# Split float32 products: one 512-column matmul for both halves of the activations

## The chip, the cores and the metric

One core of one Trainium2 chip runs the whole program. The metric is device time in microseconds, the median of several executions; lower is better.

## The reference

Two models in a row on 256 tokens of width 1024, in float32. The first block is a mixer (convolution branch, SSM branch, gates) followed by a mixture of 64 experts; the second is two layers, each with three mixing branches, an output projection and a feed-forward net with a squared ReLU. The places that matter here:

```python
# first block, end of the mixer
y_cv = u @ w_cv_out
y_ssm = y.reshape(bsz, seq, D_INNER) @ w_ssm_out
return (g_cv * y_cv + g_ssm * y_ssm) @ w_mix_out
# second block, each of two layers
x = x + merged @ w_out[l]
h2 = rms_norm(x, norm2_g[l])
x = x + jnp.square(jax.nn.relu(h2 @ w_ff1[l])) @ w_ff2[l]
```

## The kernel before

Activations are kept transposed: 128 channels on the partitions, T = 256 tokens along the free dimension; a tile is 128x256. A weight matrix is the stationary operand in blocks of 128x128. Most products are plain float32 (`group`, L176). The products named above are *split products*: a float32 weight tile is split into a high half `wh` (rounded to the one-pass type fp32r by an ACT copy) and a low half `wl` (the rest, by a DVE subtraction), the activations likewise into `xh` and `xl`, and wh*xh + wl*xh + wh*xl is summed in one PSUM bank.

**A split product** has 8 k-tiles (16 in the SSM projection) of three matmuls of 256 columns: L483 to L485 in the mixer's tail (`mixer_pe`, `halved_product`), L1724 to L1726 in the layers (`layer_pe`, `halved_product`). It fills half a bank, `k.pb[b][:, 0:T]`:

```python
e.matmul(k.pb[b][:, 0:T], wh[:, kt, c0:c0 + 128], xh, start=(first and kt == 0), stop=False)
e.matmul(k.pb[b][:, 0:T], wl[:, kt, c0:c0 + 128], xh, start=False, stop=False)
ins = e.matmul(k.pb[b][:, 0:T], wh[:, kt, c0:c0 + 128], xl, start=False, stop=(last and kt == 7))
```

**Groups and queues.** Each engine's instruction list is written out by hand and runs in order; semaphores tie the engines. In a layer the split weights come in 18 groups j of 2 MB: j = 0 and 1 the output projection, 2 to 9 `w_ff1`, 10 to 17 `w_ff2`; a group of weights serves four products. Two buffers `parts` hold the split weights. SP loads group j + 2 into the raw buffer once `ff_low` of group j is done. At the start of turn j, ACT issues `ff_high(j + 1)` (two copies of 128x2048, L1798), which waits until the products of group j - 1 are done, and DVE issues `ff_low(j + 1)` (two subtractions of 128x2048, L1805). Then both work on the four products of group j, and PE starts group j + 1 when its `ff_low` is done.

**Emptying a bank in ff1** (j = 2 to 9): ACT writes relu (L2009), DVE first makes the low half of the product before (`hid_low`, L2296) and then squares relu (L2327), ACT makes the high half (`hid_high`, L2011):

```python
o.done(e.activation(v.relu[:, m % 2, :], k.pb[k.bank["ff", 72 * l + 8 + m]][:, 0:T], ACT.Relu), k.s("relu"))
e.wait_ge(*k.at("hid_sq", 32 * l + m + 1))
o.done(e.activation(v.high[m], v.hsq[:, m % 2, :], ACT.Copy), k.s("hid_high"))
```

In the output projection and in `w_ff2` DVE adds the bank to `k.h` (L2319, L2333), ACT squares the result for the next norm (L194) and PE sums the squares (L201). PE takes banks from a ring of seven; a bank is used again when the operation that emptied it has signalled.

**The mixer's tail** has the same scheme: 8 groups, 24 products (2, 2, 2, 2 of 16 k-tiles, then 4, 4, 4, 4 of 8), `tail_high` (L644) and `tail_low` (L653) for the weights. Products 0 to 7 are multiplied by a gate when emptied (L825), 8 to 15 multiplied by a gate and added (L827, L828) and split (`yc_high` L613, `yc_low` L812); products 16 to 23 take the result as their input and go into `k.h` (L832). Just ahead of products 0 to 3 DVE finishes `uc_low` (L808), the input of products 8 to 15.

Of the kernel before, what the change touches and what calls it, by code (L numbers as in the profile page):

```python
# [215 lines left out]


# [75 lines left out]
class Mix:  # L293


    def __init__(self, k):
# [45 lines left out]
def mixer_pe(k, e, emptied):  # L342
# [133 lines left out]
    def halved_product(n, w, c0, x, kt, late):  # L476

        b = ring.take(("tail", n))
        (wl, wh), (xl, xh) = w, x
        for j in range(kt):  # L480
            if late:
                e.wait_ge(*k.at(late, 8 * j // kt + 1))
            e.matmul(k.pb[b][:, 0:T], wh[:, j, c0:c0 + 128], xh[:, j, :], start=(j == 0), stop=False)  # L483
            e.matmul(k.pb[b][:, 0:T], wl[:, j, c0:c0 + 128], xh[:, j, :], start=False, stop=False)  # L484
            ins = e.matmul(k.pb[b][:, 0:T], wh[:, j, c0:c0 + 128], xl[:, j, :], start=False, stop=(j == kt - 1))  # L485
        ins.then_inc(k.s("mm_tail"), 1)
        return b
# [168 lines left out]
def mixer_ve(k, e, o):  # L656
# [158 lines left out]
    for j in range(8):  # L815
# [4 lines left out]
        for n in range(TAIL_GROUPS[j - 1] if j else 0, TAIL_GROUPS[j]):  # L820
            acc = k.pb[k.bank["tail", n]][:, 0:T]
            e.wait_ge(*k.at("mm_tail", n + 1))
            m = n % 8
            if n < 8:
                o.done(e.tensor_tensor(m_.yc[:, m, :], acc, g[:, 8 + m, :], ALU.mult), k.s("tail"))  # L825
            elif n < 16:
                t = o.done(e.tensor_tensor(m_.tmp[:, m % 2, :], acc, g[:, m, :], ALU.mult), k.s("tail"))  # L827
                o.done(o.after(t).tensor_tensor(m_.yc[:, m, :], m_.yc[:, m, :], m_.tmp[:, m % 2, :], ALU.add), k.s("yc"))  # L828
                if m:
                    yc_low(m - 1)  # L830
            else:
                o.done(e.scalar_tensor_tensor(k.h[:, m, :], acc, k.mod[:, 16 + m:17 + m], k.h[:, m, :], ALU.mult, ALU.add), k.s("tail"))  # L832
# [510 lines left out]
class Layer:  # L1343


    def __init__(self, k, l):
# [41 lines left out]
        self.relu, self.hsq = k.tiles(80, 2), k.tiles(82, 2)  # L1388
# [93 lines left out]
def layer_pe(k, e, l, emptied_by):  # L1482
# [233 lines left out]
    def halved_product(b, j, i, x, first, last, late=None, late_from=0):  # L1716
# [767 lines left out]
```

## Time and profile before

| | us |
|---|---|
| median of 3 runs | 2615.01 (2614.14 to 2616.16) |
| the profiled execution | 2613.7 |
| its span, first to last instruction | 2611.9 |
| PE busy | 2179.4 (83%) |
| DVE busy | 1026.4 (39%) |
| ACT busy | 679.0 (26%) |
| mean granted TensorE clock | 0.908 |

The profiled execution's time is 1.8 us more than its span. A clock of 1.0 is 2.4 GHz, 0.5 is 1.2 GHz. PE is the matrix engine and PEld its weight loads, DVE the vector engine, ACT the scalar engine. An engine's busy time counts overlapping matmuls once. The split products run from 390 to 490 us (mixer's tail), 1825 to 2048 (layer 0) and 2385 to 2606 (layer 1); between lie the experts, whose weights stream from memory, and the plain float32 parts.

### The profile page before, as it was taken

How to read it: one execution, taken by the hardware profiler on the slowest of the kernel's cores; microseconds unless marked ns; L12 is line 12 of the kernel's file. 1: busy time of each engine (PE TensorE's matmuls, PEld its weight loads, DVE VectorE, ACT ScalarE, POOL GpSimd, SP SyncE). 2: the span in 40 equal slices, each digit the busy share in tenths (PEclk: the TensorE clock that was granted, in tenths of full speed). 3: DMA queues.
4: the chain of work that ended last, by engine and by line, in shares of the span. 5: the costliest groups of instructions: out<-in, count | busy, mean ns of one | idle time of the engine just before them, and what ended most of it. 6: DMA issues, size and time to landing. Idle time of an engine off the chain costs nothing.

```text
span 2611.9 us, 31851 instructions
## 1 busy us (share of the span) xinstructions
PE 2179.4 (83%) x13027; PEld 1589.9 (61%) x13027; DVE 1026.4 (39%) x2106; ACT 679.0 (26%) x1048; POOL 27.3 (1%) x47
## 2 busy tenths in 40 slices
PE   7999999867667666777666588989899988899999
PEld 4886679833223333333333265778899855688999
DVE  1577865510010000101000246763664267653653
ACT  2125665300000000000000123641453125522542
POOL 0000000000000000000000010000000200000000
PEclk8999999887887888788888799999999989899999
DMA  8443544499999999999999613233355322143452
GB/s 323 150 143 133 196 155 162 198 396 421 422 389 421 421 421 421 421 421 421 421 420 422 255 48 122 99 111 129 133 190 189 114 83 104 65 160 131 158 177 101
DMA packets 174501, 631.45 MB, mean 242 GB/s; under 512 B 10816, under 2 KB 28768, under 8 KB 125200
## 3 DMA queue, kind: packets, MB, share of 16 engines
q1 hardware_dynamic: 173008, 628.07, 61.1%
q8 instruction: 106, 1.74, 0.3%
q0 software_dynamic: 1344, 1.28, 0.3%
q14 instruction: 43, 0.35, 0.0%
HBM read 628.28 MB, written 1.05 MB: 241 GB/s over the span
## 4 chain that ended last, share of the span: by engine, by line
PE 55%; DMA 27%; DVE 10%; ACT 4%; SPq 2%; issue 2%; DVEq 0%; ACTq 0%
DMA ring<-in_w 26%; PE pb L176 23%; PE pb L1724 5%; PE pb L1725 5%; PE pb L1726 5%; PE pb L1022 4%; PE pb L1048 3%; SPq L935 2%; DVE ar L2231 1%; PE pb L485 1%; PE pb L484 1%; PE pb L483 1%; PE pb L1681 1%; DMA ring<-in_w_ada 1%; PE pb L201 1%
## 5 line engine op out<-in xcount | busy, mean ns | idle before, releaser
L176 PE MATMUL pb<-ar,ring 128*128 128x256 f32 (+1 forms) x2960 | 673.5, 387 | 32.1 <-DVE ar L2033 18.0
L176 PEld LDWEIGHTS pb<-ar,ring 128*128 128x128 f32 (+1 forms) x2960 | 561.4, 192 | 138.6 <-issue 43.6
L1022 PE MATMUL pb<-ring,ar 128*32 128x512 f32 x2048 | 283.7, 710 | 125.0 <-DMA ring<-in_w 124.4
L1724 PE MATMUL pb<-act,parts 128*128 128x256 f32 x1152 | 331.2, 287 | 13.3 <-DVE act L2309 13.3
L1725 PE MATMUL pb<-act,parts 128*128 128x256 f32 x1152 | 327.7, 284 | 0.0
L1726 PE MATMUL pb<-act,parts 128*128 128x256 f32 x1152 | 327.6, 284 | 0.0
L1048 PE MATMUL pb<-ring,ar 128*32 128x512 f32 x1024 | 174.2, 842 | 114.2 <-DMA ring<-in_w 114.2
L1022 PEld LDWEIGHTS pb<-ring,ar 128*32 128x32 f32 x2048 | 77.6, 127 | 309.7 <-issue 309.0
L1724 PEld LDWEIGHTS pb<-act,parts 128*128 128x128 f32 x1152 | 221.7, 192 | 14.5 <-issue 14.1
L1725 PEld LDWEIGHTS pb<-act,parts 128*128 128x128 f32 x1152 | 221.6, 192 | 0.4
L1726 PEld LDWEIGHTS pb<-act,parts 128*128 128x128 f32 x1152 | 221.6, 192 | 0.0
L1805 DVE TENSOR_TENSOR parts<-ring,parts 128x2048 fp32r<-128x2048 f32 x72 | 161.7, 2288 | 107.0 <-ACT parts L1798 107.0
L1048 PEld LDWEIGHTS pb<-ring,ar 128*32 128x32 f32 x1024 | 46.3, 147 | 230.1 <-issue 226.4
L1245 DVE TENSOR_TENSOR ar<-ar,pb 128x512 f32<-128x512 f32 x16 | 11.0, 687 | 432.4 <-PE pb L1022 432.4
L1099 ACT ACTIVATE ar<-pb 128x512 f32<-128x512 f32 x16 | 9.6, 597 | 598.8 <-PE pb L1048 598.8
L176 PE MATMUL pb<-ar 128*128 128x128 f32 x512 | 126.5, 423 | 44.7 <-DVE ar L1222 42.5
L176 PEld LDWEIGHTS pb<-ar 128*128 128x128 f32 x512 | 123.4, 335 | 59.0 <-DVE ar L1222 56.7
L1798 ACT ACTIVATE parts<-ring 128x2048 fp32r<-128x2048 f32 x72 | 133.5, 1901 | 79.4 <-PE pb L1726 76.6
L1253 DVE COPY ar<-pb 128x512 f32<-128x512 f32 x16 | 11.1, 692 | 277.8 <-PE pb L1048 277.8
L693 DVE SCALAR_TENSOR_TENSOR ar<-ar,par 128x256 f32<-128x256 f32 x240 | 104.5, 476 | 0.0
L1093 ACT ACTIVATE ar<-pb 128x512 f32<-128x512 f32 x16 | 9.6, 597 | 319.8 <-PE pb L1022 319.8
L176 PE MATMUL pb<-ring,ar 128*128 128x512 f32 (+3 forms) x304 | 75.3, 427 | 14.4 <-DVE ring L2148 14.4
(355 smaller groups left out, 2393.4 us busy)
## 6 DMA issues: line engine op xcount, KB each, us to landing
ring<-in_w SPq DMA_DIRECT2D x384, 1024.0 KB, 18.7
ring<-in_w_in SPq DMA_DIRECT2D x36, 2048.0 KB, 7.7
ring<-in_w_ff SPq DMA_DIRECT2D x32, 2048.0 KB, 8.7
ring<-in_w_ada SPq DMA_DIRECT2D x12, 2048.0 KB, 12.1
ring<-in_w_ssm_out SPq DMA_DIRECT2D x4, 2048.0 KB, 8.2
ring<-in_w_out SPq DMA_DIRECT2D x4, 2048.0 KB, 7.7
ring<-in_w_cv_out SPq DMA_DIRECT2D x2, 2048.0 KB, 8.2
ring<-in_w_mix_out SPq DMA_DIRECT2D x2, 2048.0 KB, 7.6
```

What stands on the lines that cost most here:

```text
L176: ins = e.matmul(out, l, r, start=(i == 0), stop=(i == len(pairs) - 1))
L201: e.matmul(k.pb[SUMS][:, 0:T], k.con("ones"), k.tiles(85 + g % 2, 1)[:, 0, :], start=first, stop=last).then_inc(k.s("squared_sum"), 1)
L483: e.matmul(k.pb[b][:, 0:T], wh[:, j, c0:c0 + 128], xh[:, j, :], start=(j == 0), stop=False)
L693: made[m] = o.done(e.scalar_tensor_tensor(uc[:, m, :], ut[:, m, j:j + T], cw[:, m, j:j + 1], uc[:, m, :], ALU.mult, ALU.add), k.s("taps") ...
L935: e.dma_start(half_slot(k, n, [128, kt, 2048 // kt]), src).then_inc(k.s(f"expert{n % HALVES}"), 16)
L1022: ins = e.matmul(k.pb[b][32 * j:32 * j + 32, :], v.xg[i][:, kt, 32 * j:32 * j + 32], w[j][:, m, :], start=(kt == 0), stop=(kt == 7))
L1048: ins = e.matmul(k.pb[yb[c]][32 * j:32 * j + 32, :], v.ht[i][:, kt, 32 * j:32 * j + 32], w[j][:, m, 512 * c:512 * c + 512], start=(kt == 0 ...
L1724: e.matmul(k.pb[b][:, 0:T], wh[:, kt, c0:c0 + 128], xh, start=(first and kt == 0), stop=False)
L1725: e.matmul(k.pb[b][:, 0:T], wl[:, kt, c0:c0 + 128], xh, start=False, stop=False)
L1726: ins = e.matmul(k.pb[b][:, 0:T], wh[:, kt, c0:c0 + 128], xl, start=False, stop=(last and kt == 7))
L1798: o.done(o.e.activation(high[:, 4 * i:4 * i + 4, :], raw[:, 4 * i:4 * i + 4, :], ACT.Copy), k.s("ff_high"))
L1805: o.done(o.e.tensor_tensor(low[:, 4 * i:4 * i + 4, :], raw[:, 4 * i:4 * i + 4, :], high[:, 4 * i:4 * i + 4, :].bitcast(F32), ALU.subtract) ...
```

## The change

The high and low halves of a tile of activations become one moving operand of 512 columns (`pair`, two tiles at a distance). `wh` multiplies both at once into a full bank of 512 columns, and `wl` multiplies the high half into the columns where wh*xh stands. The bank then holds two partial sums, which are added when it is emptied.

```diff
--- before.py
+++ after.py
@@ -214,6 +214,27 @@
     return k.tiles(88, 1)[:, 0, :]
+class Both:
+    def __init__(self, k, high, low):
+        a, b = min(high, low), max(high, low)
+        self.pair, self.high, self.at = k.act[:, a:b + 1:b - a, :], k.act[:, high, :], T * (high > low)
+def halved_products(e, acc, wh, wl, x, first, last):
+    both = acc[:, :].rearrange("p (t n) -> p t n", t=2)
+    if last:
+        e.matmul(acc[:, x.at:x.at + T], wl, x.high, start=False, stop=False)
+        return e.matmul(both, wh, x.pair, start=first, stop=True)
+    e.matmul(both, wh, x.pair, start=first, stop=False)
+    return e.matmul(acc[:, x.at:x.at + T], wl, x.high, start=False, stop=False)
 FIRST_FILLS = 2
@@ -310,7 +331,11 @@
         self.xdt = [k.scratch(9 + 4 * i, 1024).rearrange("p (t h c) -> p t h c", t=2, h=8) for i in range(2)]
         self.ucl, self.uch, self.zl, self.zh = k.act[:, 8:16, :], k.act[:, 72:80, :], k.act[:, 40:56, :], k.act[:, 24:40, :]
         self.yc, self.tmp = k.tiles(16, 8), k.tiles(82, 2)
+        self.tmp2 = k.tiles(80, 2)
         self.ycl, self.ych = k.act[:, 16:24, :], k.act[:, 0:8, :]
+        self.zb = [Both(k, 24 + m, 40 + m) for m in range(16)]
+        self.ucb = [Both(k, 72 + m, 8 + m) for m in range(8)]
+        self.ycb = [Both(k, m, 16 + m) for m in range(8)]
 def halves(k, j, shape):
@@ -476,24 +501,22 @@
     def halved_product(n, w, c0, x, kt, late):
         b = ring.take(("tail", n))
-        (wl, wh), (xl, xh) = w, x
+        wl, wh = w
         for j in range(kt):
             if late:
                 e.wait_ge(*k.at(late, 8 * j // kt + 1))
-            e.matmul(k.pb[b][:, 0:T], wh[:, j, c0:c0 + 128], xh[:, j, :], start=(j == 0), stop=False)
-            e.matmul(k.pb[b][:, 0:T], wl[:, j, c0:c0 + 128], xh[:, j, :], start=False, stop=False)
-            ins = e.matmul(k.pb[b][:, 0:T], wh[:, j, c0:c0 + 128], xl[:, j, :], start=False, stop=(j == kt - 1))
+            ins = halved_products(e, k.pb[b], wh[:, j, c0:c0 + 128], wl[:, j, c0:c0 + 128], x[j], j == 0, j == kt - 1)
         ins.then_inc(k.s("mm_tail"), 1)
         return b
     for j in range(8):
         e.wait_ge(*k.at("low", 2 * j + 2))
         if j < 4:
-            w, x, cols, kt, late = halves(k, j, [16, 256]), (m_.zl, m_.zh), 2, 16, "z_low"
+            w, x, cols, kt, late = halves(k, j, [16, 256]), m_.zb, 2, 16, "z_low"
         elif j < 6:
-            w, x, cols, kt, late = halves(k, j, [8, 512]), (m_.ucl, m_.uch), 4, 8, "uc_low"
+            w, x, cols, kt, late = halves(k, j, [8, 512]), m_.ucb, 4, 8, "uc_low"
         else:
-            w, x, cols, kt, late = halves(k, j, [8, 512]), (m_.ycl, m_.ych), 4, 8, "yc_low"
+            w, x, cols, kt, late = halves(k, j, [8, 512]), m_.ycb, 4, 8, "yc_low"
         for i in range(cols):
             n = (TAIL_GROUPS[j - 1] if j else 0) + i
             b = halved_product(n, w, 128 * i, x, kt, late)
@@ -818,18 +841,25 @@
         if 2 <= j < 7:
             tail_low(k, o, j + 1)
         for n in range(TAIL_GROUPS[j - 1] if j else 0, TAIL_GROUPS[j]):
-            acc = k.pb[k.bank["tail", n]][:, 0:T]
+            acc = [k.pb[k.bank["tail", n]][:, T * i:T * i + T] for i in range(2)]
             e.wait_ge(*k.at("mm_tail", n + 1))
             m = n % 8
+            tmp = m_.tmp[:, m % 2, :]
             if n < 8:
-                o.done(e.tensor_tensor(m_.yc[:, m, :], acc, g[:, 8 + m, :], ALU.mult), k.s("tail"))
+                o.done(e.tensor_tensor(m_.yc[:, m, :], acc[0], g[:, 8 + m, :], ALU.mult))
+                t = o.done(e.tensor_tensor(tmp, acc[1], g[:, 8 + m, :], ALU.mult), k.s("tail"))
+                o.done(o.after(t).tensor_tensor(m_.yc[:, m, :], m_.yc[:, m, :], tmp, ALU.add))
             elif n < 16:
-                t = o.done(e.tensor_tensor(m_.tmp[:, m % 2, :], acc, g[:, m, :], ALU.mult), k.s("tail"))
-                o.done(o.after(t).tensor_tensor(m_.yc[:, m, :], m_.yc[:, m, :], m_.tmp[:, m % 2, :], ALU.add), k.s("yc"))
+                t1 = o.done(e.tensor_tensor(tmp, acc[0], g[:, m, :], ALU.mult))
+                t2 = o.done(e.tensor_tensor(m_.tmp2[:, m % 2, :], acc[1], g[:, m, :], ALU.mult), k.s("tail"))
+                t1 = o.done(o.after(t1).tensor_tensor(tmp, tmp, m_.yc[:, m, :], ALU.add))
                 if m:
                     yc_low(m - 1)
+                o.done(o.after(t1, t2).tensor_tensor(m_.yc[:, m, :], tmp, m_.tmp2[:, m % 2, :], ALU.add), k.s("yc"))
             else:
-                o.done(e.scalar_tensor_tensor(k.h[:, m, :], acc, k.mod[:, 16 + m:17 + m], k.h[:, m, :], ALU.mult, ALU.add), k.s("tail"))
+                h, gain = k.h[:, m, :], k.mod[:, 16 + m:17 + m]
+                t = o.done(e.scalar_tensor_tensor(h, acc[0], gain, h, ALU.mult, ALU.add))
+                o.done(o.after(t).scalar_tensor_tensor(h, acc[1], gain, h, ALU.mult, ALU.add), k.s("tail"))
 def mixer_po(k, e):
@@ -1385,7 +1415,10 @@
         self.nh, self.nl = k.act[:, 8:16, :], k.act[:, 16:24, :]
         self.high = [k.act[:, 24 + m, :] for m in range(32)]
         self.low = [k.act[:, (56 + m if m < 24 else m - 24), :] for m in range(32)]
-        self.relu, self.hsq = k.tiles(80, 2), k.tiles(82, 2)
+        self.hid, self.hsq, self.part = k.tiles(80, 2), k.tiles(82, 2), k.tiles(91, 2)
+        self.mgb = [Both(k, 68 + m, 60 + m) for m in range(8)]
+        self.nb = [Both(k, 8 + m, 16 + m) for m in range(8)]
+        self.hidb = [Both(k, 24 + m, 56 + m if m < 24 else m - 24) for m in range(32)]
 def unit_place(v, name):
@@ -1718,12 +1751,9 @@
         wl, wh = halves(k, j, [8, 512])
         c0 = 128 * i
         for kt in range(8):
-            xl, xh = x(kt)
             if late:
                 e.wait_ge(*k.at(late, late_from + kt + 1))
-            e.matmul(k.pb[b][:, 0:T], wh[:, kt, c0:c0 + 128], xh, start=(first and kt == 0), stop=False)
-            e.matmul(k.pb[b][:, 0:T], wl[:, kt, c0:c0 + 128], xh, start=False, stop=False)
-            ins = e.matmul(k.pb[b][:, 0:T], wh[:, kt, c0:c0 + 128], xl, start=False, stop=(last and kt == 7))
+            ins = halved_products(e, k.pb[b], wh[:, kt, c0:c0 + 128], wl[:, kt, c0:c0 + 128], x[kt], first and kt == 0, last and kt == 7)
         ins.then_inc(k.s("mm_ff"), 1)
     mid = SQ[f"mid{l}"]
@@ -1733,7 +1763,7 @@
             m = 4 * j + i
             b = wide.take(("ff", 72 * l + m))
             if j < 2:
-                halved_product(b, j, i, lambda kt: (v.mgl[:, kt, :], v.mgh[:, kt, :]), True, True, "mg_low", 8 * l)
+                halved_product(b, j, i, v.mgb, True, True, "mg_low", 8 * l)
                 wide.until(b, *k.at("h_mid", 8 * l + m + 1))
                 if m >= 2:
                     square_sum(k, e, mid + m - 2, ROOT[f"mid{l}"], m == 2, False)
@@ -1741,8 +1771,8 @@
                     square_sum(k, e, mid + 6, ROOT[f"mid{l}"], False, False)
                     square_sum(k, e, mid + 7, ROOT[f"mid{l}"], False, True)
             else:
-                halved_product(b, j, i, lambda kt: (v.nl[:, kt, :], v.nh[:, kt, :]), True, True, "n_low", 8 * l)
-                wide.until(b, *k.at("relu", 32 * l + m - 7))
+                halved_product(b, j, i, v.nb, True, True, "n_low", 8 * l)
+                wide.until(b, *k.at("hid", 32 * l + m - 7))
     for half in range(2):
         bs = [wide.take(("ff2", 8 * l + 4 * half + i)) for i in range(4)]
         for kb in range(4):
@@ -1750,7 +1780,7 @@
             e.wait_ge(*k.at("ff_low", 2 * (NSPLIT * l + j + 1)))
             e.wait_ge(*k.at("hid_low", 32 * l + 8 * kb + 8))
             for i in range(4):
-                halved_product(bs[i], j, i, lambda kt: (v.low[8 * kb + kt], v.high[8 * kb + kt]), kb == 0, kb == 3)
+                halved_product(bs[i], j, i, v.hidb[8 * kb:8 * kb + 8], kb == 0, kb == 3)
                 if kb == 3:
                     m = 4 * half + i
                     wide.until(bs[i], *k.at("h_out", 8 * l + m + 1))
@@ -2005,8 +2035,8 @@
                 m -= 8
                 e.wait_ge(*k.at("mm_ff", 72 * l + 8 + m + 1))
                 if m >= 2:
-                    e.wait_ge(*k.at("hid_sq", 32 * l + m - 1))
-                o.done(e.activation(v.relu[:, m % 2, :], k.pb[k.bank["ff", 72 * l + 8 + m]][:, 0:T], ACT.Relu), k.s("relu"))
+                    e.wait_ge(*k.at("hid", 32 * l + m - 1))
+                o.done(e.activation(v.part[:, m % 2, :], k.pb[k.bank["ff", 72 * l + 8 + m]][:, T:2 * T], ACT.Copy), k.s("part"))
                 e.wait_ge(*k.at("hid_sq", 32 * l + m + 1))
                 o.done(e.activation(v.high[m], v.hsq[:, m % 2, :], ACT.Copy), k.s("hid_high"))
             elif l == 0 and j in (13, 17):
@@ -2295,6 +2325,11 @@
         e.wait_ge(*k.at("hid_high", 32 * l + m + 1))
         return o.done(e.tensor_tensor(v.low[m], v.hsq[:, m % 2, :], v.high[m].bitcast(F32), ALU.subtract), k.s("hid_low"))
+    def add_halves(m, b, told):
+        h = k.h[:, m, :]
+        t = o.done(e.tensor_tensor(h, k.pb[b][:, 0:T], h, ALU.add))
+        o.done(o.after(t).tensor_tensor(h, k.pb[b][:, T:2 * T], h, ALU.add), k.s(told))
     low_done = [None, None]
     for j in range(NSPLIT):
         if j == 0:
@@ -2316,21 +2351,23 @@
             m = 4 * j + i
             if j < 2:
                 e.wait_ge(*k.at("mm_ff", 72 * l + m + 1))
-                o.done(e.tensor_tensor(k.h[:, m, :], k.pb[k.bank["ff", 72 * l + m]][:, 0:T], k.h[:, m, :], ALU.add), k.s("h_mid"))
+                add_halves(m, k.bank["ff", 72 * l + m], "h_mid")
             elif j < 10:
                 m -= 8
+                acc, hid = k.pb[k.bank["ff", 72 * l + 8 + m]], v.hid[:, m % 2, :]
+                e.wait_ge(*k.at("part", 32 * l + m + 1))
+                t = o.done(e.tensor_tensor(hid, acc[:, 0:T], v.part[:, m % 2, :], ALU.add), k.s("hid"))
                 if m:
                     low_done[(m - 1) % 2] = hid_low(m - 1)
-                e.wait_ge(*k.at("relu", 32 * l + m + 1))
                 if m >= 2:
                     o.after(low_done[m % 2])
-                o.done(e.tensor_tensor(v.hsq[:, m % 2, :], v.relu[:, m % 2, :], v.relu[:, m % 2, :], ALU.mult), k.s("hid_sq"))
+                o.done(o.after(t).scalar_tensor_tensor(v.hsq[:, m % 2, :], hid, 0.0, hid, ALU.max, ALU.mult), k.s("hid_sq"))
                 if m == 31:
                     hid_low(31)
             elif j in (13, 17):
                 m = 4 * (j // 17) + i
                 e.wait_ge(*k.at("mm_ff", 72 * l + (56 if j == 13 else 72) - 3 + i))
-                o.done(e.tensor_tensor(k.h[:, m, :], k.pb[k.bank["ff2", 8 * l + m]][:, 0:T], k.h[:, m, :], ALU.add), k.s("h_out"))
+                add_halves(m, k.bank["ff2", 8 * l + m], "h_out")
     if l:
         for n in range(4):
             if n % 2:
```

## Rows read from the trace of the kernel before

**Rows 1.** The page, busy time and share of the span: PE.
```profile
PE 2179.4 (83%) x13027; PEld 1589.9 (61%) x13027; DVE 1026.4 (39%) x2106; ACT 679.0 (26%) x1048; POOL 27.3 (1%) x47
```

**Rows 2.** The page, chain that ended last, by line: shares of the span.
```profile
DMA ring<-in_w 26%; PE pb L176 23%; PE pb L1724 5%; PE pb L1725 5%; PE pb L1726 5%; PE pb L1022 4%; PE pb L1048 3%; SPq L935 2%; DVE ar L2231 1%; PE pb L485 1%; PE pb L484 1%; PE pb L483 1%; PE pb L1681 1%; DMA ring<-in_w_ada 1%; PE pb L201 1%
```

**Rows 3.** Busy time by stage: layer 0, groups 2 to 9, and four microseconds of it.
```profile
core 0: us, PE busy (x) PEld busy (x) DVE busy (x) ACT busy (x) POOL busy (x), PEclk, DMA share, GB/s
1858.60:1953.30 94.70, 94.54 (x771) 94.57 (x772) 61.81 (x86) 51.57 (x80) 0.00 (x0) 0.97 0.46 166
1859.00:1863.00 4.00, 4.00 (x20) 4.00 (x21) 4.00 (x7) 3.33 (x2) 0.00 (x0) 0.50 0.01 2
```

**Rows 4.** Timeline of ACT, one group of ff1: start, length, instruction [idle before].
```profile
1931.39 3.71 ACT L1798 ACTIVATE parts<-ring 128x2048 fp32r<-128x2048 f32 x2
...
1938.59 0.42 ACT L2011 ACTIVATE act<-ar 128x256 fp32r<-128x256 f32 x1 [3.23 <-DVE ar L2327]
1938.91 0.37 ACT L2009 ACTIVATE ar<-pb 128x256 f32<-128x256 f32 x1
...
1942.58 0.42 ACT L2011 ACTIVATE act<-ar 128x256 fp32r<-128x256 f32 x1 [0.49 <-DVE ar L2327]
1942.90 1.90 ACT L1798 ACTIVATE parts<-ring 128x2048 fp32r<-128x2048 f32 x1
```

**Rows 5.** Timeline of DVE, the same group.
```profile
1937.80 0.42 DVE L2296 TENSOR_TENSOR act<-ar,act 128x256 fp32r<-128x256 f32 x1
1938.14 0.42 DVE L2327 TENSOR_TENSOR ar<-ar 128x256 f32<-128x256 f32 x1
...
1939.38 0.42 DVE L2327 TENSOR_TENSOR ar<-ar 128x256 f32<-128x256 f32 x1
```

**Rows 6.** Groups of instructions, shapes apart: count, busy us, mean ns, idle before.
```profile
L1724 PE MATMUL pb<-act,parts 128*128 128x256 f32 x1152 | 331.2, 287 | 13.3 <-DVE act L2309 13.3
...
L483 PE MATMUL pb<-act,parts 128*128 128x256 f32 x256 | 73.7, 288 | 0.0
...
L1724 PEld LDWEIGHTS pb<-act,parts 128*128 128x128 f32 x1152 | 221.7, 192 | 14.5 <-issue 14.1
...
L2264 DVE TENSOR_TENSOR ar<-ar 128x512 f32<-128x512 f32 x2 | 1.4, 684 | 0.0
...
L2267 DVE SCALAR_TENSOR_TENSOR ar<-ar 128x512 f32<-128x512 f32 x2 | 1.4, 682 | 0.0
```

**Rows 7.** The chain of work in order of time: start, length of the piece, what.
```profile
1740.43 1.72 PE pb L1660 x4
1742.15 82.88 PE pb L176 x384
...
1860.59 0.21 PE pb L1725
```

**Rows 8.** Timeline of PE: matmuls of one column, and the last transposes.
```profile
204.04 0.95 PE L337 MATMUL pb<-const,ring 128*128 128x1 f32 x8
...
2606.11 1.94 PE L171 MATMUL pb<-const,h 128*128 128x128 f32 x16 [0.61 <-DVE h L2333]
```

**Rows 9.** Timeline of DVE, mixer's tail: products 0 to 3, 5, 12, 15.
```profile
420.31 1.41 DVE L825 TENSOR_TENSOR ar<-pb,ar 128x256 f32<-128x256 f32 x4
...
430.24 0.42 DVE L825 TENSOR_TENSOR ar<-pb,ar 128x256 f32<-128x256 f32 x1 [3.64 <-PE pb L485]
...
460.86 0.42 DVE L827 TENSOR_TENSOR ar<-pb,ar 128x256 f32<-128x256 f32 x1
461.31 0.42 DVE L828 TENSOR_TENSOR ar<-ar 128x256 f32<-128x256 f32 x1
...
466.17 0.43 DVE L812 TENSOR_TENSOR act<-ar,act 128x256 fp32r<-128x256 f32 x1 [0.15 <-ACT act L613]
```

**Rows 10.** Timeline of PE in layer 1: the first matmul after an idle stretch.
```profile
2214.00 0.48 PE L176 MATMUL pb<-ar,ring 128*128 128x256 f32 x1 [2.79 <-ACT ar L1880]
```

**Rows 11.** Busy time and granted clock around that stretch, columns as in rows 3.
```profile
2210.00:2220.00 10.00, 7.21 (x33) 5.47 (x31) 8.10 (x19) 8.58 (x13) 0.00 (x0) 0.83 0.00 0
```

## The prediction

> **What bounds the kernel now.** I read the page's busy line first: PE is busy 83% of the span [rows 1]. The chain that ended last says which busy time counts [rows 2]: most is the load of MoE weights and full float32 products (L176), which the change does not touch; the reader should see that the three split products L1724 to L1726 hold 15% and L483 to L485 3%. The windows come next: in the stage of split products PE was busy 94.5 of 94.7 us at clock 0.97, DVE 61.8 and ACT 51.6 [rows 3]. So PE sets this stage, and a cheaper product seems to go straight to the time. But busy shares hide handshakes, so the timelines of ACT and DVE over one group of four products were read last [rows 4, 5]. The two `ff_high` of one group start at 1931.39, those of the next at 1942.90: 11.51 us for 96 matmuls, 0.120 each.
>
> **The matmuls.** There are 1152 + 256 = 1408 k-tiles of three [rows 6]: 0.360 us each. The change makes two matmuls of the three: 512 columns with `wh`, 256 with `wl`. Neither a 512-column nor any other size of this one-pass type is in the trace, so the pair is bounded. Float32 matmuls are recorded as two passes and take two array cycles a column: 82.88 us / 384 = 0.216 for 256 columns, 1.72 / 4 = 0.430 for 512 [rows 7]. So columns cost in proportion, and one pass of 512 one-cycle columns takes about 0.216, of 256 about 0.109 (as the 128-column two-cycle row: 1.94 us for 16, 0.109 apart after the first) [rows 8]. The measured 0.120 is more than 0.109. At the low clock of 0.5 [rows 3] the interval is 0.21 [rows 7], which is 256/1.2 with nothing added, so a fixed extra per matmul is unlikely. Loading 128 weight columns has a floor: matmuls of one column are (0.95-0.25-0.03)/6 = 0.112 apart [rows 8]. I take the 0.120 as a weight load running beside a matmul. Behind a 512-column matmul the next load is hidden, behind a 256-column one it is not: 0.216 + 0.120 = **0.336** a k-tile. Bounds: 0.325 if a load behind the short one costs only 0.109; 0.360 if 0.120 is a price per column (0.240 + 0.120), when nothing is gained. I take the middle because the floor of 0.112 lies near 0.120. A product of 8 k-tiles goes from 2.88 to 2.69 us (-0.19), a group of four from 11.52 to 10.75. All 1408 on the path would give 1408 x 0.024 = 33.8 us. They are not all on it.
>
> A load takes 0.192 us by its record, yet load and matmul repeat every 0.120 [rows 4, 6], so they run beside each other. The Trainium skill ("TensorE: Matmul & The Clock Gate", part 3, "What overlaps and what doesn't") says that a load overlaps a running matmul only when its row group differs. The trace disagrees, since all of these use all 128 rows; by the rule a dropped load would be worth its whole time, which is a rival below.
>
> **The added work in ff1** (groups j = 2 to 9, both layers). Before, for each product: ACT relu, DVE square, ACT `high`, and DVE `hid_low` of the product before. ACT and DVE wait for each other. After: ACT copies the second half (`part`), DVE adds the first (`hid`), then `hid_low`, then the square, then ACT `high`, and only then can ACT, in order, copy the next `part`. Steps, from rows: square to `high` 1938.59-1938.14 = 0.45; `high` to the next PSUM read 0.32 [rows 4, 5]; that read 0.37 and 0.03 until DVE starts = 0.40, no longer hidden behind `high`'s end; `hid` 0.335; `hid_low` to square 0.34 (1938.14-1937.80). Sum **1.85** a product against 1.24 before (1939.38-1938.14) [rows 5]. The square is now a scalar_tensor_tensor with a constant: that form takes 682 ns at 512 elements where tensor_tensor takes 684 [rows 6], so it costs nothing more.
> One turn of the loop, from one `ff_high` to the next: 6.41 until the split of the next weights lets DVE go on (1937.80-1931.39) + 0.335 + 0.34 + 3 x 1.85 + 0.45 + 0.32 = **13.4 us** [rows 4, 5]. Before, the same sum is 6.41 + 0.34 + 3 x 1.24 + 0.45 + 0.32 = 11.2, just under PE's 11.52, which is why no wait shows. After, 13.4 is over PE's 10.75: PE waits for the weights' low half, queued on DVE behind the `hid` work, and that is late next.
> How much arrives: the split has slack at first. From the last product of group 2 (E2), 1.9 to the first turn (0.04 + 0.37 + 0.03 + 0.335 + 0.34 + 0.45 + 0.32), then 7 turns of 13.4, then 6.5 to the low half of group 11, then its 10.75 and 0.2 of pipeline: E2 + 113.2. Before: 9 x 11.52 = 103.7. So **+9.5** a layer.
>
> **The rest of a layer.** Groups 0 to 2: 12 products x 0.192 = -2.3; the second DVE add at the end of the output projection is exposed, 0.42 + 0.04 = +0.46. Groups 12 to 17: 24 x 0.192 = -4.6, DVE and ACT only split weights there and the split keeps its slack. The last add: +0.46. Layer: 9.5 - 2.3 + 0.5 - 4.6 + 0.5 = +3.6, two layers **+7.2**. The wait for `part` is also queued in front of `hid_low` on DVE, but its `high` is done by then: nothing. The banks come free later, at `hid` in place of relu; a product waits for a bank used seven products earlier, so more than a group of slack covers it. DMAs are issued after `ff_low` as before, two groups ahead; the next turns are longer, so they are covered. ACT's instruction count does not change.
>
> **The mixer's tail** (256 k-tiles, products of 16 k-tiles 5.76 to 5.38). Products 0 to 3 are emptied in one go before the split for group 3: four at 0.33 become four chains mult, mult, add of 0.33 + 0.46 + 0.34 = 1.13. With products 0 to 2 done earlier this chain starts 0.8 earlier, at 419.5, the split then runs 424.1 to 428.5; PE wants it at 430.0 - 6 x 0.384 = 427.7 [rows 9]: stall 0.8. After eight products: -3.1 + 0.8 = -2.3. Products 8 to 15: a dependent pair 0.45 apart before (461.31-460.86); after, five DVE operations of 0.336 = 1.68 each. From the end of product 7: split done +6.45, four at 1.68 (+0.15 for the first), `high` 0.4, split of group 6 done at 19.7, four more, then the last `yc_low` at 27.4; product 16 needs it for its last k-tile and ends at 27.8. Before, it ended at 25.9 (9 x 2.88), the last `yc_low` starting at 466.17, half a microsecond early [rows 9]. +1.9. The other seven products -1.3, the second add at the end +0.5. Sum **-1.2**.
>
> **Sum:** 7.2 - 1.2 = +6.0 on the profiled execution's 2613.7 us (span 2611.9 and 1.8 around it). The median 2615.0 lies 1.3 above that execution: **2621.0**.
>
> **Rivals.** Faster and slower mean by over 0.2%, 5.2 us, about what a measurement of this kernel can tell.
> (a) 0.120 is per column. Then products gain nothing: a layer 10.3 + 0.5 + 0.5 = +11.3, the mixer's tail +1.9 + 0.5 = +2.4: +25, 2640. The same comes if the operand of two separate tiles is fetched more slowly or goes out as two instructions. For it: 0.120 is above the load's floor. Against: that floor is near. 20%.
> (b) 0.325 a k-tile: layer +9.2 - 3.4 + 0.5 - 6.7 + 0.5 = about 0, mixer -2: 2613, no change. 10%.
> (c) Faster: ACT and DVE are limited by work and not by the handshake. DVE's own work in a group is 4.4 + 4 x 1.01 = 8.5 us, ACT's 3.6 + 4 x 0.7 = 6.4, both under 10.75. Then PE sets ff1 too: a layer 72 x -0.192 + 0.9 = -12.9, the mixer -5.6: -31, 2584. It decides if the round is below (10.75 - 6.41 - 0.675 - 0.77)/3 = 0.96 us. Against it: even today's round is 1.24, and DVE waits for ACT and ACT for DVE in each. 5%.
> (d) A dropped load is worth its whole 0.112: 0.248 a k-tile, product 1.98. The loop of 13.4 still caps ff1: layer 6.7 - 10.3 - 21.0 = -24.6, mixer about -8: 2558. 1%. The overlap rule of the Trainium skill's page named above would bring this.
> (e) The clock: PE now idles 13.4 - 10.75 = 2.7 us in each turn. After an idle of 2.79 us at 2211 the ten microseconds around it had a mean clock of 0.83, so 3.4 us at the low level [rows 10, 11], 1.7 us lost, less than the 2.7 it idles. Twice as long costs 3.4, 0.7 more than the idle, in some 12 turns: +9, 2630. 6%.
>
> **How the numbers follow.** The forecast of 2621 has 58%. Its own error, 0.05 us in each step of the loop, is +-3 us, so some 18% of it lies under 2620.2 and is "same". With (b): same 0.28. Faster is (c), (d) and a little of (b): 0.08. Slower: 0.64. The range takes in (b) and (a): 2612 to 2640; (c) and (d) and tails are left out.
>
> **What the profile will show.** 1408 matmuls of 512 columns 0.216 apart from the next, 1408 of 256 at 0.120; `ff_high` pairs 13.4 us apart in groups 4 to 9, `part` starting 0.32 after `high`; PE waiting 2 to 3 us per group for L1805's line, none in groups 12 to 17; one PE wait of 3 to 4 us for the last `yc_low` in the mixer's tail. Wrong would be: 0.240 between long matmuls (a), turns of about 11 us (c), or a clock under 0.9 in ff1 (e).

## The result, and the profile after

| | before | after |
|---|---|---|
| median, us | 2615.59 (4 runs) | 2635.44 (4 runs, 2633.33 to 2637.39) |
| ratio to before | 1 | 1.0076, 95% interval 1.0064 to 1.0088 |
| profiled execution | 2613.7 | 2633.3 |
| its span | 2611.9 | 2631.5 |

The changed kernel is slower by 20 us, 0.76%. The page after, busy time and the chain by line:

```profile
PE 2167.4 (82%) x11619; PEld 1513.3 (58%) x11619; DVE 1073.5 (41%) x2242; ACT 677.0 (26%) x1048; POOL 27.3 (1%) x47
...
DMA ring<-in_w 26%; PE pb L176 22%; PE pb L232 7%; PE pb L1078 3%; PE pb L1052 3%; PE pb L233 3%; DVE parts L1835 3%; SPq L965 2%; ACT parts L1828 1%; DVE ar L2261 1%; PE pb L1714 1%; DVE ar L2364 1%; DVE ar L2359 1%; DMA ring<-in_w_ada 1%; PE pb L201 1%
```

There are 1408 fewer matmuls than in [rows 1], yet PE's busy time fell by 12 us only, and the chain has new members that [rows 2] has not: the weight split L1835 (`ff_low`, L1805 before), its ACT part L1828, the square L2364 and the new add L2359. The shapes, as in [rows 6]:

```profile
L232 PE MATMUL pb<-act,parts 128*128 128x512 f32 x1288 | 474.4, 408 | 30.2 <-DVE parts L1835 13.6 <-DVE act L2344 13.3 <-DVE act L2326 2.0
L233 PE MATMUL pb<-act,parts 128*128 128x256 f32 x1288 | 365.6, 284 | 0.0
...
L231 PE MATMUL pb<-act,parts 128*128 128x512 f32 x120 | 47.6, 397 | 0.0
L230 PE MATMUL pb<-act,parts 128*128 128x256 f32 x120 | 34.0, 283 | 0.6 <-DVE act L835 0.6
```

1288 + 120 = 1408 pairs, in one instruction each, as the change says. A long matmul, however, is not followed by the next at 0.216 us. The timeline of PE in ff1 of layer 0 (start, length, instruction, idle before):

```profile
1938.89 0.40 PE L232 MATMUL pb<-act,parts 128*128 128x512 f32 x1
1939.12 0.28 PE L233 MATMUL pb<-act,parts 128*128 128x256 f32 x1
1939.24 0.39 PE L232 MATMUL pb<-act,parts 128*128 128x512 f32 x1
...
1951.83 0.50 PE L232 MATMUL pb<-act,parts 128*128 128x512 f32 x1 [1.93 <-DVE parts L1835]
```

The starts are 0.235 and 0.117 apart (medians over all of them), 0.352 a k-tile: 0.008 less than the 0.360 of the three, not 0.024. The last row is PE's new wait at the start of a group, for the low half of its weights.

Where the 20 us are, by stage. Layers 0 and 1 of the changed kernel, from the end of group 0 to the ends of groups 2, 11 and 17 (busy time of PE, PEld, DVE, ACT, POOL, then the clock):

```profile
1841.20:1876.40 35.20, 27.97 (x144) 23.68 (x143) 23.59 (x39) 16.54 (x25) 0.00 (x0) 0.90 0.41 142
1876.40:1990.20 113.80, 105.89 (x578) 90.73 (x577) 75.60 (x127) 55.97 (x82) 0.00 (x0) 0.97 0.48 166
1990.20:2060.10 69.90, 69.90 (x395) 60.70 (x395) 29.91 (x34) 21.42 (x17) 0.00 (x0) 1.00 0.43 150
2408.00:2443.10 35.10, 27.87 (x143) 23.60 (x142) 23.59 (x39) 16.54 (x26) 0.00 (x0) 0.90 0.40 142
2443.10:2556.80 113.70, 106.03 (x577) 90.67 (x576) 71.88 (x106) 52.65 (x76) 0.00 (x0) 0.97 0.47 165
2556.80:2624.60 67.80, 67.80 (x385) 58.56 (x383) 28.22 (x24) 18.60 (x10) 0.00 (x0) 1.00 0.28 99
```

and the same stretches of layer 0 before:

```profile
1837.20:1872.50 35.30, 28.51 (x208) 27.48 (x207) 20.98 (x32) 16.65 (x25) 0.00 (x0) 0.90 0.40 145
1872.50:1976.20 103.70, 103.70 (x867) 103.70 (x866) 65.04 (x90) 56.80 (x82) 0.00 (x0) 1.00 0.49 176
1976.20:2047.40 71.20, 71.20 (x588) 70.94 (x587) 28.13 (x34) 21.41 (x17) 0.00 (x0) 1.00 0.43 154
```

The middle stretch carries it: 103.7 with PE busy all of it before, 113.8 with PE idle for 7.9 after. The stretch behind it is 1.3 shorter, the one ahead the same. From the end of group 0 to the end of group 17, layer 0 took 8.7 us more and layer 1 8.8. The mixer's tail, from the end of its first product to the end of its last, took 95.4 against 93.4, +2.0. The rest of the span adds up to +0.1: +0.2 ahead of the tail, +1.8 from the tail to layer 0 (mostly the stretch of experts, where the DMA engines are busy 0.99 of the time in both kernels, 948.5 us against 947.0), -2.4 between the layers (no run explains this one), +0.5 at the end, where the second add is exposed.

The turn of ACT and DVE in ff1, one group, to be laid beside [rows 4] and [rows 5]. ACT:

```profile
1945.28 3.71 ACT L1828 ACTIVATE parts<-ring 128x2048 fp32r<-128x2048 f32 x2
1948.89 0.35 ACT L2039 ACTIVATE ar<-pb 128x256 f32<-128x256 f32 x1
1952.81 0.42 ACT L2041 ACTIVATE act<-ar 128x256 fp32r<-128x256 f32 x1 [3.56 <-DVE ar L2364]
1953.13 0.36 ACT L2039 ACTIVATE ar<-pb 128x256 f32<-128x256 f32 x1
1954.65 0.42 ACT L2041 ACTIVATE act<-ar 128x256 fp32r<-128x256 f32 x1 [1.16 <-DVE ar L2364]
...
1958.34 0.42 ACT L2041 ACTIVATE act<-ar 128x256 fp32r<-128x256 f32 x1 [1.16 <-DVE ar L2364]
1958.67 3.70 ACT L1828 ACTIVATE parts<-ring 128x2048 fp32r<-128x2048 f32 x2
```

and DVE:

```profile
1947.28 4.49 DVE L1835 TENSOR_TENSOR parts<-ring,parts 128x2048 fp32r<-128x2048 f32 x2 [2.36 <-ACT parts L1828]
1951.69 0.41 DVE L2359 TENSOR_TENSOR ar<-pb,ar 128x256 f32<-128x256 f32 x1
1952.03 0.41 DVE L2326 TENSOR_TENSOR act<-ar,act 128x256 fp32r<-128x256 f32 x1
1952.36 0.42 DVE L2364 SCALAR_TENSOR_TENSOR ar<-ar 128x256 f32<-128x256 f32 x1
1953.53 0.42 DVE L2359 TENSOR_TENSOR ar<-pb,ar 128x256 f32<-128x256 f32 x1 [0.75 <-ACT ar L2039]
1953.87 0.41 DVE L2326 TENSOR_TENSOR act<-ar,act 128x256 fp32r<-128x256 f32 x1
1954.20 0.42 DVE L2364 SCALAR_TENSOR_TENSOR ar<-ar 128x256 f32<-128x256 f32 x1
```

The reader should see three things. From one `ff_high` to the next: 1958.67 - 1945.28 = 13.39 us, against 11.51 in [rows 4]. From square to square: 1954.20 - 1952.36 = 1.84, against 1.24. And no engine is full: in each round DVE is idle 0.75 while ACT copies the second half, and ACT 1.16 while DVE adds, subtracts and squares.

### The profile page after: what moved, and what is told of

Same layout as the page of the kernel before. It is cut to its first block, busy times and chain, and to the rows that moved or that the text cites. A ratio compares the mean times of both kernels' runs of the same rounds, so it can differ in the third digit from the quotient of the medians.

```text
span 2631.5 us, 29179 instructions
## 1 busy us (share of the span) xinstructions
PE 2167.4 (82%) x11619; PEld 1513.3 (58%) x11619; DVE 1073.5 (41%) x2242; ACT 677.0 (26%) x1048; POOL 27.3 (1%) x47
## 4 chain that ended last, share of the span: by engine, by line
PE 46%; DMA 27%; DVE 17%; ACT 6%; issue 3%; SPq 2%; DVEq 0%; ACTq 0%
DMA ring<-in_w 26%; PE pb L176 22%; PE pb L232 7%; PE pb L1078 3%; PE pb L1052 3%; PE pb L233 3%; DVE parts L1835 3%; SPq L965 2%; ACT parts L1828 1%; DVE ar L2261 1%; PE pb L1714 1%; DVE ar L2364 1%; DVE ar L2359 1%; DMA ring<-in_w_ada 1%; PE pb L201 1%
## 5 line engine op out<-in xcount | busy, mean ns | idle before, releaser
L232 PE MATMUL pb<-act,parts 128*128 128x512 f32 x1288 | 474.4, 408 | 30.2 <-DVE parts L1835 13.6
L1052 PE MATMUL pb<-ring,ar 128*32 128x512 f32 x2048 | 277.6, 697 | 126.7 <-DMA ring<-in_w 126.1
L233 PE MATMUL pb<-act,parts 128*128 128x256 f32 x1288 | 365.6, 284 | 0.0
L232 PEld LDWEIGHTS pb<-act,parts 128*128 128x128 f32 x1288 | 246.8, 192 | 90.9 <-DVE parts L1835 16.8
L1078 PE MATMUL pb<-ring,ar 128*32 128x512 f32 x1024 | 173.2, 838 | 120.9 <-DMA ring<-in_w 120.9
L233 PEld LDWEIGHTS pb<-act,parts 128*128 128x128 f32 x1288 | 248.0, 193 | 4.4
L1835 DVE TENSOR_TENSOR parts<-ring,parts 128x2048 fp32r<-128x2048 f32 x72 | 161.7, 2288 | 97.4 <-ACT parts L1828 97.2
L1828 ACT ACTIVATE parts<-ring 128x2048 fp32r<-128x2048 f32 x72 | 133.5, 1902 | 70.1 <-PE pb L233 59.7
L1283 DVE COPY ar<-pb 128x512 f32<-128x512 f32 x16 | 11.1, 691 | 283.5 <-PE pb L1078 283.5
L1260 DVE COPY ar<-pb 128x512 f32<-128x512 f32 x32 | 22.1, 691 | 116.2 <-PE pb L176 116.2
L176 PEld LDWEIGHTS pb<-ring,ar 128*128 128x128 f32 (+1 forms) x304 | 41.2, 182 | 43.6 <-issue 37.7
```

Source lines behind the costliest of these rows:

```text
L176: ins = e.matmul(out, l, r, start=(i == 0), stop=(i == len(pairs) - 1))
L232: e.matmul(both, wh, x.pair, start=first, stop=False)
L233: return e.matmul(acc[:, x.at:x.at + T], wl, x.high, start=False, stop=False)
L1052: ins = e.matmul(k.pb[b][32 * j:32 * j + 32, :], v.xg[i][:, kt, 32 * j:32 * j + 32], w[j][:, m, :], start=(kt == 0), stop=(kt == 7))
L1078: ins = e.matmul(k.pb[yb[c]][32 * j:32 * j + 32, :], v.ht[i][:, kt, 32 * j:32 * j + 32], w[j][:, m, 512 * c:512 * c + 512], start=(kt == 0 ...
L1828: o.done(o.e.activation(high[:, 4 * i:4 * i + 4, :], raw[:, 4 * i:4 * i + 4, :], ACT.Copy), k.s("ff_high"))
```

## The experiments

Three questions were open: is the loss the turn in ff1, or spread; is it the order or the amount of the added work; and why does the long matmul take 0.235.

### Only ff1 back to three matmuls

```diff
+            if 2 <= j < 10:
+                e.matmul(k.pb[b][:, 0:T], wh[:, kt, c0:c0 + 128], x[kt].high, start=(kt == 0), stop=False)
+                e.matmul(k.pb[b][:, 0:T], wl[:, kt, c0:c0 + 128], x[kt].high, start=False, stop=False)
+                ins = e.matmul(k.pb[b][:, 0:T], wh[:, kt, c0:c0 + 128], x[kt].low, start=False, stop=(kt == 7))
...
-                t = o.done(e.tensor_tensor(hid, acc[:, 0:T], v.part[:, m % 2, :], ALU.add), k.s("hid"))
+                o.done(e.tensor_tensor(v.hsq[:, m % 2, :], v.part[:, m % 2, :], v.part[:, m % 2, :], ALU.mult), k.s("hid_sq"))
```

> Only ff1 goes back to three matmuls of 256 columns and to relu and square; all else as changed. Theory HANDSHAKE (the turn of ACT and DVE in ff1 caps it at 13.4 us): ff_high to ff_high falls from 13.4 to 11.5, PE's waits in ff1 go; per layer 40 products x -0.06 and two adds of 0.46 = -1.6, mixer's tail +2.2, so 2615.6 - 3.2 + 2.2 = 2614.6. Rival SPREAD (the second add and the later release of banks cost everywhere, ff1 is only a part): over 2625.

Measured: 2614.0 us, ratio 0.9991 (0.9982 to 1.0001), as the theory of the handshake had it (2614.6); the spread theory had over 2625. From one `ff_high` to the next it is 11.52 us again, and the layers took 208.4 and 206.3, less than the 210.2 and 207.8 before. With 512 of the 1408 pairs undone all of the loss is gone, and 1.5 us are won, less than can be told from nothing.

### The same operations, the copy earlier

```diff
-                e.wait_ge(*k.at("mm_ff", 72 * l + 8 + m + 1))
-                if m >= 2:
-                    e.wait_ge(*k.at("hid", 32 * l + m - 1))
-                o.done(e.activation(v.part[:, m % 2, :], k.pb[k.bank["ff", 72 * l + 8 + m]][:, T:2 * T], ACT.Copy), k.s("part"))
+                for n in ([m] if i == 0 else []) + ([m + 1] if i < 3 else []):
+                    e.wait_ge(*k.at("mm_ff", 72 * l + 8 + n + 1))
+                    if n >= 2:
+                        e.wait_ge(*k.at("hid", 32 * l + n - 1))
+                    o.done(e.activation(v.part[:, n % 2, :], k.pb[k.bank["ff", 72 * l + 8 + n]][:, T:2 * T], ACT.Copy), k.s("part"))
                 e.wait_ge(*k.at("hid_sq", 32 * l + m + 1))
```

> ACT copies the second half of product m + 1 before it waits for the square of product m; same operations, same count, same matmuls as changed. HANDSHAKE: a round falls from 1.84 to 1.24 us (the copy is off the round trip, what is left is square, high, hid_low), the turn from 13.4 to 6.41 + 0.335 + 0.34 + 3 x 1.24 + 0.45 + 0.32 = 11.6, just over PE's 11.28; per layer -2.6 in groups 3 to 11, -0.3 before and -1.1 behind them, so 2615.6 - 8.0 + 2.2 = about 2610. Rival WORK (the added operations themselves fill DVE or ACT): turn stays near 13.4, 2635.

Measured: 2613.1 us, ratio 0.9990 (0.9981 to 1.0000). ACT of this kernel, the same view as above:

```profile
1940.55 3.70 ACT L1828 ACTIVATE parts<-ring 128x2048 fp32r<-128x2048 f32 x2
1944.16 0.63 ACT L2040 ACTIVATE ar<-pb 128x256 f32<-128x256 f32 x2
1948.09 0.42 ACT L2042 ACTIVATE act<-ar 128x256 fp32r<-128x256 f32 x1 [3.29 <-DVE ar L2365]
1948.41 0.36 ACT L2040 ACTIVATE ar<-pb 128x256 f32<-128x256 f32 x1
1949.33 0.42 ACT L2042 ACTIVATE act<-ar 128x256 fp32r<-128x256 f32 x1 [0.56 <-DVE ar L2365]
...
1952.15 1.90 ACT L1828 ACTIVATE parts<-ring 128x2048 fp32r<-128x2048 f32 x1
```

Two copies stand ahead of the first `high`, and the `high`s are 1949.33 - 1948.09 = 1.24 apart, as expected; ACT's idle time in a round is back from 1.16 to 0.56. The turn is 1952.15 - 1940.55 = 11.60 us, the expected 11.6. That is still a little over PE's 11.28, but PE waits for no split of weights in groups 3 to 11: the lead that the split has at the start of ff1 lasts. Every operation of the changed kernel is still there. So the order costs, not the work. Layers 0 and 1 (end of group 0 to end of group 17, by windows) took 205.9 and 204.2 us, against 210.2 and 207.8 before and 218.9 and 216.6 changed. The median came out 3 us above the expected 2610. The tail is not the reason, since by its windows the changed one costs 1.9 and 2.2 were allowed for (next). In the profiled execution the experts' stretch took 949.1 us against 947.0 before; the rest is within what the ten runs of this kernel differ by (2610.6 to 2617.7).

### Only the mixer's tail back to three matmuls

```diff
-            ins = halved_products(e, k.pb[b], wh[:, j, c0:c0 + 128], wl[:, j, c0:c0 + 128], x[j], j == 0, j == kt - 1)
+            e.matmul(k.pb[b][:, 0:T], wh[:, j, c0:c0 + 128], xh[:, j, :], start=(j == 0), stop=False)
+            e.matmul(k.pb[b][:, 0:T], wl[:, j, c0:c0 + 128], xh[:, j, :], start=False, stop=False)
+            ins = e.matmul(k.pb[b][:, 0:T], wh[:, j, c0:c0 + 128], xl[:, j, :], start=False, stop=(j == kt - 1))
...
-                t2 = o.done(e.tensor_tensor(m_.tmp2[:, m % 2, :], acc[1], g[:, m, :], ALU.mult), k.s("tail"))
```

> Only the mixer's tail goes back to three matmuls and its old emptying; layers as changed. The wait of PE at product 16 (4.4 us by the profile) goes; mixer's tail back by 2.2 us: 2633.2. Rival: product 16 waits for something else and the tail's time stays.

Measured: 2629.9 us, ratio 1.0058 (1.0039 to 1.0076): 5.5 us below the changed kernel in the medians, where 2.2 were expected. By windows the tail itself gives back 95.4 - 93.5 = 1.9. The waits that it removes are these, from PE's timeline of the changed kernel at product 16, its k-tiles 5, 6 and 7 waiting for `yc_low` (L835):

```profile
465.66 0.49 PE L232 MATMUL pb<-act,parts 128*128 128x512 f32 x1 [0.27 <-DVE act L835]
...
467.33 0.50 PE L232 MATMUL pb<-act,parts 128*128 128x512 f32 x1 [1.05 <-DVE act L835]
...
468.57 0.39 PE L230 MATMUL pb<-act,parts 128*128 128x256 f32 x1 [0.64 <-DVE act L835]
```

That the other 3 us are real is not shown. The two profiled executions differ by 2.4 (2633.3 and 2630.9), the runs of this kernel go from 2627.9 to 2636.5, its interval overlaps that of the changed kernel (1.0064 to 1.0088), and the old tail was worth 2.5 us where the early copy was in place (2613.1 against 2610.6, last experiment). One difference outside the tail does repeat: the experts' matmuls ran over 947.0 to 947.2 us in the three kernels with the old tail, and over 948.3 to 949.6 in all eight that were profiled with the new one. Why the experts' stretch should differ at all was not tried.

### The added emptying alone

```diff
+    if not first:
+        e.matmul(acc[:, x.at:x.at + T], wh, x.high, start=False, stop=False)
+        e.matmul(acc[:, x.at:x.at + T], wl, x.high, start=False, stop=False)
+        return e.matmul(acc[:, T - x.at:2 * T - x.at], wh, x.low, start=False, stop=last)
```

> Banks, halves and emptying as changed, but from the second k-tile on the pair is again two matmuls of 256 columns. This is the added emptying alone, with nearly nothing gained on PE (0.360 a k-tile). The prediction's rival (a) gave 2640 for it: layers +11.3 each, mixer's tail +2.4. If the theory of the turn is right: turns of 13.4 in ff1 and about 2640; the pairing itself is then worth about 5 us with the turn in place. If the changed kernel's loss came from the long matmul itself: about 2615.

Measured: 2641.6 us, ratio 1.0094 (1.0078 to 1.0109); turns of 13.4 again, matmuls 0.120 apart. So emptying two halves costs 26 us where nothing is gained on PE, and the pairing gives about 6 us of it back with the turn in place (5 by the ratios; the two intervals overlap a little, 1.0078 to 1.0109 and 1.0064 to 1.0088).

### Is it the distance of the two tiles?

```diff
-        self.nh, self.nl = k.act[:, 8:16, :], k.act[:, 16:24, :]
+        self.nh, self.nl = k.act[:, 8:23:2, :], k.act[:, 9:24:2, :]
...
-        self.hidb = [Both(k, 24 + m, 56 + m if m < 24 else m - 24) for m in range(32)]
+        self.hidb = [Both(k, at[m], at[m] + 1) for m in range(32)]
```

> In both layers the high and low half of an activation tile of ff1 and ff2 stand beside each other, so that the moving operand is one run of 512 columns; the output projection and the mixer's tail keep two distant tiles. Theory DISTANCE (the 0.235 us of the long matmul comes from fetching two distant tiles): the long matmuls of ff1 and ff2 come down to 0.216, those of the output projection stay at 0.235; ff2 shortens by 32 products x 8 x 0.019 = 4.9 us a layer, time about 2625. Theory STREAM (a column of this type costs 0.459 ns wherever it lies): 0.235 everywhere, time 2635 as with the change.

Measured: 2636.2 us, ratio 1.0083 (1.0065 to 1.0100). The 944 long matmuls that read one run of 512 are 0.236 us from the next, the 344 that read two tiles 0.236 too. The distance costs nothing.

### Fewer weight columns, fewer moving columns

```diff
+    wh, wl = wh[:, 0:64], wl[:, 0:64]
+    if three:
+        e.matmul(acc[0:64, 0:T], wh, x.high, start=first, stop=False)
...
+    both = acc[0:64, :].rearrange("p (t n) -> p t n", t=2)
```

> In ff2 the weights are 64 columns in place of 128 (the rest of each output tile is left out); layer 0 uses three matmuls of 256 columns there, layer 1 the pair. Theory LOADS (the time over the array's own 0.109 and 0.216 comes from weight loads that share a port with the moving operand): layer 0 goes from 0.120 to about 0.109, layer 1 from 0.235 to about 0.22 and from 0.117 to 0.109. Theory STREAM (the moving operand of this type comes in at about 2.2 columns a ns, whatever is loaded): 0.120 in layer 0 and 0.235, 0.117 in layer 1 stay.

> As weights64 with 32 weight columns in ff2 (three matmuls of 256 in layer 0, the pair in layer 1; the rest of each output tile is left out). 128 and 64 columns gave 0.120 and 0.113 for three; 0.235 + 0.117 and 0.228 + 0.112 for the pair. If each weight column costs 0.1 ns: 0.110 in layer 0, and 0.224 + 0.109 in layer 1, so that some 8 ns of the long matmul are not the loads'. If the long matmul's whole excess over 0.213 is the loads': it falls to 0.219 or less.

> In ff2 the long matmul (but for the first k-tile of each product) takes 2 x 192 = 384 columns in layer 0 and 2 x 128 = 256 in layer 1; the other columns are left out. Per column and a small fixed part (0.449 ns a column and 5 ns, from 0.120 and 0.235): 384 take 0.177 and 256 in two pieces 0.120. If the excess over the array is fixed per long matmul (0.235 - 0.213 = 0.022): 0.182 and 0.129.

These kernels leave out a part of each product of ff2 and were executed once each, so their whole times say nothing here; the layers' ff2 is read. PE's timeline in layer 1, first 64, then 32 weight columns:

```profile
2560.16 0.39 PE L238 MATMUL pb<-act,parts 128*64 128x512 f32 x1
2560.39 0.27 PE L239 MATMUL pb<-act,parts 128*64 128x256 f32 x1
2560.50 0.39 PE L238 MATMUL pb<-act,parts 128*64 128x512 f32 x1
```

```profile
2560.16 0.39 PE L238 MATMUL pb<-act,parts 128*32 128x512 f32 x1
2560.39 0.28 PE L239 MATMUL pb<-act,parts 128*32 128x256 f32 x1
2560.50 0.40 PE L238 MATMUL pb<-act,parts 128*32 128x512 f32 x1
```

Medians of the distance from one start to the next, in ns:

| weight columns | three of 256 | long (512) | short behind it |
|---|---|---|---|
| 128 | 120 | 235 | 117 |
| 64 | 113 | 228 | 112 |
| 32 | 113 and 118, two clusters | 229 and 234, two clusters | 117 |

| long matmul of | distance | short behind it |
|---|---|---|
| 2 x 128 | 120 | 120 |
| 2 x 192 | 176 | 117 |
| 2 x 256 | 235 | 117 |

With half the weight columns every matmul, long or short, came 5 to 7 ns sooner after the one before, so neither pure theory holds. But a quarter of the columns took no more off, and part of it came back. With 32 columns the distance even changes within one stage, while the instructions stay the same. Starts of k-tiles in layer 0 of that kernel, around 2000 and 2030 us:

```profile
1999.82 0.28 PE L231 MATMUL pb<-act,parts 128*32 128x256 f32 x1
...
2000.17 0.28 PE L231 MATMUL pb<-act,parts 128*32 128x256 f32 x1
...
2029.76 0.28 PE L231 MATMUL pb<-act,parts 128*32 128x256 f32 x1
...
2030.10 0.28 PE L231 MATMUL pb<-act,parts 128*32 128x256 f32 x1
```

The median k-tile of three took 353 ns up to about 2012 us and 340 from there to about 2046. With 64 columns it was 340 for most of the stage, and 360 around 2012 us and again near its end. So something besides the load moves the distance by as much as halving the load did, and narrower weights also fill less of the array and write fewer rows of the bank. That weight loads slow a running matmul is therefore not shown. Nor is the bundling worth anything at 64 columns: the median k-tile is 340 ns as three matmuls and 340 as a pair.

Over moving columns the price is near to 0.45 ns a column plus 5, as the expectation had it (0.120 and 0.177). At the low clock, where a column takes 0.83 ns, the distances of the changed kernel are 427 and 213 ns, the array's own and nothing more. So this one-pass type costs 0.46 ns a column at the full clock in pairs and 0.47 in threes, loads included; what holds it back stays open.

### Both repairs together

The early copy in the layers and the old mixer's tail.

> The early copy in the layers and the old mixer's tail together. Layers -3.9 and -3.7 against before as the early copy showed (205.9 and 204.2 us from the first group's end against 210.2 and 207.8), tail 0: 2615.5 - 8.0 = 2607.6. If a part of the gain is given back outside the stages: 2611 or more.

Measured: 2610.6 us over 11 runs, ratio 0.9981 (0.9972 to 0.9990): 4.6 us below the kernel before and 25 below the changed one. It lies between the 2607.6 that the stages alone give and the 2611 of the second expectation. The windows of its profiled execution:

```profile
395.50:488.90 93.40, 93.23 (x747) 90.81 (x746) 50.93 (x69) 41.17 (x52) 0.00 (x0) 1.00 0.50 185
1836.30:2042.90 206.60, 199.37 (x1113) 172.58 (x1113) 129.17 (x199) 93.86 (x124) 0.00 (x0) 0.98 0.47 166
2394.10:2599.00 204.90, 197.65 (x1103) 171.09 (x1101) 123.78 (x169) 87.73 (x111) 0.00 (x0) 0.98 0.42 149
```

The tail is at 93.4 as before and the layers at 206.6 and 204.9, 3.6 and 2.9 below before. The expectation had 3.9 and 3.7 (and the numbers that it names for layer 0, 210.2 and 205.9, give 4.3), so a part of the gain is missing in the layers themselves. It is the fastest of the kernels that compute every product in full.

## Why the prediction was right, and where it was not

**The sign and its cause were right.** The turn of 13.4 us was worked out from the rows of before and measured at 13.39, the round of 1.85 at 1.84, the square as scalar_tensor_tensor at 0.42 like the tensor_tensor that it replaced. Undoing ff1 alone removed the loss, and moving one copy did too, so this cause is shown and not only argued.

**The size was not.** I forecast +6 us (2621.0), and 2635.4 was measured, +20. It lies in the range up to 2640 only because rival (a), at 20%, was taken in: in part that is luck, as the middle forecast was 14 us off.

**The step that failed is the price of the matmul pair.** I took 0.336 a k-tile, because I read the 0.120 between short matmuls as a wait for the weight load, which a long matmul would hide. The bound above it, 0.360, was nearly right: 0.352 was measured. Of the 13.6 us between the forecast and the profiled execution this price makes 10 in the layers, and the mixer's tail makes 3.2. The argument that the floor of 0.112 for loads "lies near" 0.120 was weak: the two differ by 8 ns, and the array's own 0.107 differs from 0.120 by no more than 13. Two numbers close to a third do not say which of them sets it. With 64 weight columns the short matmuls would have had to fall to the array's pace if loads alone held them; most stopped at 0.113, and the long ones at 0.228.

Put into the prediction's own sum, 0.352 gives: groups 0 to 2 12 x -0.064 + 0.5 = -0.3; groups 3 to 11 9.5 + 0.5 = +10.0; groups 12 to 17 24 x -0.064 + 0.5 = -1.1. That is +8.6 a layer. The windows leave out group 0 (-0.3) and the last add (+0.5), so 8.4 is to be laid beside the 8.7 and 8.8 measured. Group by group: +10.1 for groups 3 to 11 (113.8 against 103.7), -1.3 behind them, about 0 ahead. PE waited 0.3 to 1.9 us for its weights, five times a layer, and not 2 to 3, since a group takes it 11.28 us and not 10.75.

**The mixer's tail.** Forecast -1.2, measured +2.0; with the price corrected the products save 0.13 us (16 k-tiles) or 0.06 each, 2.0 in all and not 6. The wait for the last `yc_low` came where it was put: product 16 ended 28.1 us after product 7 (27.8 forecast). It was split over k-tiles 5 to 7, since each `yc_low` is waited for by itself. Against nine products of 2.82 that is +2.7. A further +1.0 I had missed: product 19 ended 4.5 us after product 18, 3.5 before, because PE's first sum of squares stands ahead of it and the second adds, behind the last split of weights on DVE, come later. The stall of 0.8 before product 6 did not come, because PE was not early enough for it. The split itself ended at 429.2, later than the 428.5 forecast: its chain did not start 0.8 earlier, since DVE finished `uc_low` ahead of it at 420.3, as before. -2.0 + 2.7 + 1.0 = +1.7, of the 2.0 measured.

**The rivals.** (a), the price per column, is what happened for the most part; its 2640 is what the kernel with unpaired matmuls took (2641.6). (b) and (d) fell with the matmul's price. (c), ff1 at PE's pace, fell with the turn of 13.39; the early copy confirms that the handshake made it, with the same work and no loss. (e), the clock: in groups 3 to 11 it was 0.97 against 1.00 before, and twice in each layer it fell to 0.5 right behind one of PE's waits. But the clock's loss fell into time in which PE would have waited: the wait at L1835 is 1.93 us in one turn and 0.35 in the one before, in which the clock was low, and the turn stays 13.4 either way. PE's ten waits at L1835 are 13.6 us in all. So of the price that the rival gave, 0 to 9, none shows.

**The rule on weight loads.** The prediction named the rule of the Trainium skill ("TensorE: Matmul & The Clock Gate", part 3, "What overlaps and what doesn't") that a load overlaps a running matmul only when its row group differs. The trace before already spoke against it, and the result agrees with the trace: the pair, with one load less, was worth 8 ns a k-tile, far from the 112 of a load by itself.

## What to carry to other kernels

Two engines that are busy 54% and 65% of a stage, as ACT and DVE were here [rows 3], can be one step from setting its pace: add up one turn of the loop through all engines that wait for each other, and compare it with the bound engine's turn, before adding an operation to it. Here 11.2 against 11.5 us left room for nothing, and one copy in the wrong place cost 20 us while the same copy one place earlier cost none. Bundle matmuls for what a column costs, not for the loads saved, unless a run has shown that loads hold them back.

## What the runs showed that I had not expected

A one-pass float32 matmul at the full clock costs 0.46 to 0.47 ns a moving column where the two-pass float32 of the same kernel costs 0.42 a column and cycle (0.430 us for 512 columns of two cycles, [rows 7]). At the low clock both run at the array's pace: 213 ns for 256 columns of the one, 427 for 256 of the other. Half the weight columns brought the matmuls 5 to 7 ns closer together. A quarter brought less in most of the stage, in two clusters that no change of the instructions explains.
